# Gate halves copied out of PSUM between the silu groups, and the gated product written phase by phase

## The reference, cut to what matters

```python
h = rms_norm(x, mix_norm_g[l])
proj = h @ w_in[l]
a, gl, u_pool, g_conv, g_pool = jnp.split(proj, split_at, axis=-1)
yc = a * jax.nn.sigmoid(gl)                              # the gated product, 512 channels
yc = causal_dwconv(yc, conv_dw_w[l]) + conv_dw_b[l]      # 31 taps
yc = jax.nn.silu(layer_norm(yc, conv_ln_g[l], conv_ln_b[l]))
yc = yc @ w_conv_out[l]
zp = multiscale_pool(u_pool)
yp = jnp.einsum("bsgc,gcd->bsgd", zp, w_pool_grp[l]).reshape(b, s, d) * pool_scale[l]
merged = jax.nn.sigmoid(g_conv) * yc + jax.nn.sigmoid(g_pool) * yp
x = x + merged @ w_out[l]
```

## Time and profile before

| | us |
|---|---|
| median of three runs | 4167.49 |
| the three runs | 4167.48, 4446.34, 4167.49 |
| the profiled execution | 4192.85 |
| its slowest core (3), first to last instruction | 4191.3 |
| its other cores | 4155.9 to 4190.1 |
| TensorE busy | 3937.4 (94%) |
| VectorE busy | 2655.0 (63%) |
| ScalarE busy | 1983.3 (47%) |
| GpSimd busy | 203.6 (5%) |

### The profile page before, as it was taken

The page is one execution under the profiler, slowest core; times in us unless marked ns, Lnnn a source line. Parts: engine busy times, 40 slices in busy tenths (PEclk is TensorE's granted clock), DMA queues, the critical chain, the costliest instruction groups (busy, mean ns, idle before and its releaser), DMA issues.

```text
span 4191.3 us, 56900 instructions; the slowest of 8 cores (4155.9 to 4191.3 us)
## 1 busy us (share of the span) xinstructions
PE 3937.4 (94%) x18320; PEld 1797.1 (43%) x18320; DVE 2655.0 (63%) x3240; ACT 1983.3 (47%) x3793; POOL 203.6 (5%) x379
## 2 busy tenths in 40 slices
PE   6999999999999999989999999999999989999898
PEld 2444444444443444434444444444444434444343
DVE  4537775377764876548775387653867549665576
ACT  3445435454454543445444464434645445453544
POOL 1000001000000000000010000100000000000000
PEclk9899999999999999999999999999999999999999
DMA  6552353534752336333574434534257524352242
GB/s 129 111 91 49 67 94 71 91 53 78 145 126 51 66 64 106 66 55 52 101 153 101 85 52 80 94 65 85 51 111 141 105 44 76 67 98 53 53 76 68
DMA packets 108816, 348.20 MB, mean 83 GB/s; under 512 B 11888, under 2 KB 46960, under 8 KB 83952
## 3 DMA queue, kind: packets, MB, share of 16 engines
q0 software_dynamic: 41760, 275.11, 38.3%
q1 hardware_dynamic: 66768, 69.46, 6.2%
HBM read 586.05 MB, written 16.78 MB: 144 GB/s over the span
## 4 chain that ended last, share of the span: by engine, by line
PE 85%; ACT 6%; DVE 4%; issue 3%; DMA 1%; SPq 0%; DVEq 0%; ACTq 0%; POOLq 0%; POOL 0%
PE ps L424 85%; ACT F L397 2%; DVE H L411 2%; ACT AR L397 1%; ACT L397 1%; ACT RS L397 1%; DVE AR L728 1%; ACT SQ L397 1%; DVE X L401 1%; DMA AR<-xT 0%; DVE SQ L401 0%; ACT GB L397 0%; DMA RING<-wst 0%; DVE X L411 0%; DMA AR<-AR 0%
## 5 line engine op out<-in xcount | busy, mean ns | idle before, releaser
L424 PE MATMUL ps<-H,RING 128*128 128x512 bf16 x10240 | 2321.9, 386 | 97.9 <-DVE H L411 47.7
L424 PEld LDWEIGHTS ps<-H,RING 128*128 128x128 bf16 x10240 | 1012.1, 99 | 1366.4 <-issue 249.0
L424 PE MATMUL ps<-AR,RING 128*128 128x512 bf16 x4864 | 1085.1, 380 | 34.1 <-ACT RS L397 21.6
L397 ACT ACTIVATE AR<-ps 128x512 bf16<-128x512 f32 (+1 forms) x1024 | 602.6, 600 | 675.6 <-PE ps L424 648.4
L411 DVE SCALAR_TENSOR_TENSOR F<-AR,VEC,F 128x1024 f32<-128x1024 bf16 (+1 forms) x576 | 687.9, 1194 | 100.9 <-ACT F L397 58.2
L424 PEld LDWEIGHTS ps<-AR,RING 128*128 128x128 bf16 x4864 | 475.1, 98 | 614.9 <-issue 60.6
L401 DVE TENSOR_TENSOR X<-ps,X 128x512 f32<-128x512 f32 x512 | 341.4, 686 | 280.4 <-PE ps L424 280.4
L397 ACT ACTIVATE SQ<-X 128x512 bf16<-128x512 f32 x384 | 241.9, 631 | 575.0 <-DVE X L401 493.0
L397 ACT ACTIVATE GB<-ps 128x512 bf16<-128x512 f32 x320 | 184.0, 606 | 467.0 <-PE ps L424 466.2
L500 POOL DMA_DIRECT2D RING<-wst x280 | 149.0, 532 | 3687.3 <-PE ps L424 3667.9
L397 ACT ACTIVATE GB<-F 128x1024 bf16<-128x1024 f32 x192 | 189.4, 987 | 279.3 <-DVE F L411 278.4
(11 more groups left out here) (75 smaller groups left out, 2049.5 us busy)
## 6 DMA issues: line engine op xcount, KB each, us to landing
RING<-wst POOLq DMA_DIRECT2D x184, 1024.0 KB, 10.1
RING<-wst POOLq DMA_DIRECT2D x64, 704.0 KB, 8.4
RING<-wst POOLq DMA_DIRECT2D x32, 768.0 KB, 7.6
AR<-AR SPq DMA_DIRECT2D x256, 64.0 KB, 4.6
X<-xT SPq DMA_DIRECT2D x64, 256.0 KB, 14.2
yT<-X SPq DMA_DIRECT2D x64, 256.0 KB, 8.4
AR<-xT SPq DMA_DIRECT2D x40, 256.0 KB, 7.0
WX<-wst POOLq DMA_DIRECT2D x8, 1280.0 KB, 15.7
```

The costliest lines, as they stand in the source:

```text
L397: S.add("act", lambda h: h.activation(out=out.ap, in_=in_.ap, func=func, scale=s, **kw), reads=rd, writes=out.keys)
L424: S.add("pe", lambda h: h.matmul(out.ap, lhsT=lhsT.ap, rhs=rhs.ap, start=start, stop=stop), reads=lhsT.keys + rhs.keys, writes=out.keys)
```

## The change

There are two edits in the mixer.

The first changes the access patterns of the gated product (L725 to L727), and neither its inputs, its result nor its place. Before, the loops ran over n outside and the phase j inside: both inputs were read in order of position, and each of the 512 results was written 512 bytes from the one before it. Now j runs outside and n inside: the results are written in four runs of 128 neighbours, PSUM is read at every fourth float32 (16 bytes apart) and GB at every fourth bf16 (8 bytes apart).

The second moves gate halves q = 6 to 9 into the rounds of `ln_finish`. Behind the four silus and four DMAs of round r, the eight matmuls of q = 6 + r are recorded, and a Copy on ScalarE brings their bank as float32 into a half of F0 or F1 (`park`). Behind `ln_finish` four Sigmoids read the parked halves and write the same places of GB as before; then q = 10 to 15 follow as they did.

```diff
             def ev_gl(c):
                 def ev(s, ps):
                     ACT(sub(sgs[c], s), ps.v(), AF.Sigmoid)
-                    o_ap = GLU[c].ap.rearrange("p (j n) -> p n j", j=4)[:, s * 128:(s + 1) * 128, :]
-                    a_ap = psa[c].ap.rearrange("p (n j) -> p n j", j=4)
-                    g_ap = sub(sgs[c], s).ap.rearrange("p (n j) -> p n j", j=4)
+                    o_ap = GLU[c].ap.rearrange("p (j n) -> p j n", j=4)[:, :, s * 128:(s + 1) * 128]
+                    a_ap = psa[c].ap.rearrange("p (n j) -> p j n", j=4)
+                    g_ap = sub(sgs[c], s).ap.rearrange("p (n j) -> p j n", j=4)
                     S.add("dve", lambda h: h.tensor_tensor(out=o_ap, in0=a_ap, in1=g_ap, op=ALU.mult),
...
                         S.add("sp", lambda h, src=src, dst=dst: h.dma_start(out=dst, in_=src),
                               reads=YS[g].v().keys, writes=[("ACP", g)], dma_sem="ac%d" % g)
+                    gate_half(6 + q, GP[q])
+                    done.add(6 + q)
+
+            GP = [F[0].v(0, ST), F[0].v(ST, T), F[1].v(0, ST), F[1].v(ST, T)]
 
-            def gate_half(q):
+            def gate_half(q, park=None):
...
-                ACT(sub(gates[k], s), ps.v(), AF.Sigmoid)
+                if park is None:
+                    ACT(sub(gates[k], s), ps.v(), AF.Sigmoid)
+                else:
+                    ACT(park, ps.v(), AF.Copy)
+                    parked.append((sub(gates[k], s), park))
...
             ln_finish()
             if pstate.pop("x_pending", False):
                 unit_load(now["b"], hf)
-            for k in range(3, 8):
+            for o_, i_ in parked:
+                ACT(o_, i_, AF.Sigmoid)
+            for k in range(5, 8):
                 do_gate(k)
```

More of the change, by code:

```diff
@@ L862, in mixer @@
             done = set()
+            parked = []
             blk = ring_get(l, "upb")
```

## The result

| | before | changed |
|---|---|---|
| median, us | 4167.48 | 4203.0 |
| lowest and highest of the runs compared | 4166.86, 4167.49 | 4200.37, 4205.31 |
| slowest core of the profiled execution | 4191.3 (core 3) | 4203.8 (core 1) |
| waits of TensorE for the gates' sigmoid | 22.0 | none |
| waits of TensorE for the layer norm's DMAs | 1.8 | 61.3 |

The ratio is 1.0086, with a 95% interval of 1.0066 to 1.0105: 36 us slower, where 20 us less were forecast. Some executions of most kernels here, the profiled one of the kernel before with its stretch at a granted 0.81 among them, have two or four cores at a lower clock than the others; the times in this document are of executions in which all eight were alike, and so the two profiled spans differ by 12.5 us only while the runs give the 36.

A forecast was written before the change was run, and what follows sets the result against it. TensorE's chain of waits, 85% TensorE itself, was taken as the bound, with clock lost behind waits. Product 28.4 us gained, gate halves 2.1 - 4.0 - 6 = -8: 20 us off 4167.5 gives 4147 us, range 4129 to 4171.

The forecast's parts named there:

- the sentence on SP's queue: Eighth mixer, layer norm: SP's last DMA issue stays at 3772.4, lands at 3774.6; TensorE's wait moves there, 0.7 us gained.
- the clock at these places: New waits before the convolution's output, 3.0 to 4.5 us, over 5 in the fourth mixer: 6 us more charged for half clock.
- The bound at 2.43: Gated product on VectorE: 0.69 us taken; 2.43, no gain, if the new reads are as dear as the old writes.
- slower than before: Rival: strided reads hold the product up; edits cancel at 1.9 us, 4175 us at 2.43; chance 0.11, values between included.
- The last application: Even mixers: the layer norm's last application on VectorE ends at 606.14 instead of 609.24, 3.1 us earlier.
- its clock term: Even mixers: shorter half-clock stretch behind the waits gives back between 1.7 and 3.4 us a mixer, 2.55 taken.
- The product's edit: All mixers: even 22.6, first odd 2.6, bank waits of the others 3.2; 28.4 us gained, between 24 and 33.
- no table load: Rival: each Copy among the silus brings table loads on ScalarE, 10 us a mixer, 4217 us; chance 0.03. Forecast: 77 as before.
- The copies delay the last silu: Layer norm on ScalarE: four copies between silus make the last silu 1.5 us later, hidden behind SP's lag.
- The memory squares of the fourth mixer: First and fourth mixer: four copies in front on ScalarE make the squares 2.0 us later, twice, minus 4.0.
- the DMAs did not come earlier: Rival: SP issues at 0.55 us, not 0.79; last landing 2.7 us earlier in six mixers, 4131 us; chance 0.09.
- No gain, clock lost: Rival: new waits at the convolution's output all bring long slow stretches, about -20, against the product's gain; 4166 us, chance 0.15.

## Why the prediction was wrong

**The step that failed** is the sentence on SP's queue: "its last issue stays at 3772.4 and lands at 3774.6", and with it "the wait moves from the bank to the DMA, and 0.7 us is gained". The issue did stay. The landing did not: 6.9 to 8.6 us for the last four, instead of 2.2. The 2.2 were read from a stretch of the kernel before in which no weight load was in flight, and carried into one in which the edit itself puts a load of 1 MB there. The forecast followed the queues that the edit names, ScalarE's and SP's, and never asked what TensorE's earlier end of q = 15 sets free. In this kernel it frees a ring slot, and POOL's queue was waiting for nothing else: the row was in the timeline of the eighth mixer, 0.6 us after TensorE had ended q = 15. Holding this load back took 48 us off, halving it took 26: shown.

The price was in the trace of the kernel before as well. There the load that takes the slot of q = 7 is issued 3.6 us ahead of the first of the same 16 DMAs, and the first six of them take 5.1 to 7.1 us to land:

```profile
3756.74 0.53 POOL L500 DMA_DIRECT2D RING<-wst  x1 [26.94 <-PE ps L424]
```

```profile
L837 SPq DMA_DIRECT2D AR<-AR x6: 547/578/1611, 3760.3 to 3764.0; - x6
...
DMA to landing us min/median/max: 5.1/6.3/7.1
```

It cost nothing there, because the last of the 16, for which TensorE waits, come later. Over that whole trace the DMAs of L837 take 3.7 us in the median and up to 8.4.

**What followed from it** is the clock at these places, 6 us forecast. The waits went from 24 us (22.0 + 1.8) to 72 (61.3 + 10.5), and the half-clock time rose from 125 to 172 us where the product alone lowered it to 99. The halves cost 4227 - 4167.5 = 60 us. Some 41 to 46 are longer waits (68 against 27 in the median of the cores, 59.5 + 10.5 against 23.8 on core 3), and 13 are clock: TensorE works 125 us at half clock with the halves alone and 99 before. In the six mixers of the long waits the half-clock stretches of core 1 are 10.2 or 13.7 us; the part of them that lies in the wait costs nothing, as from 3782 to 3786. With the load held, TensorE works 92 us at half clock against 80 with the product alone, which is the 6 us that were forecast.

**Right in mechanism and near in size:**
- The product takes 0.69 us. The bound at 2.43 is out, and with it the rival "slower than before". What the Trainium skill ("Advanced Engine Details and Errata", section Memory Cachelines) says of PSUM lines of 8 bytes, it says of matmuls; PSUM read at a stride of 16 bytes and GB at 8 cost VectorE nothing that these rows show.
- The last application comes 3.3 us earlier (3.1 forecast), and the slow stretch at the start of the even mixers is nearly always gone, which is the upper bound of its clock term. The product's edit gave 25 us of 28.4: 15 of waits and 10 of clock, where 17 and 11 were reckoned.
- TensorE no longer stops before q = 14; no table load is added (77 as before).
- The copies delay the last silu by 1.2 us (9.42 from first start to last end against 8.20; 1.5 forecast), and SP's lag hides it.
- The memory squares of the fourth mixer start 1.9 us later behind the first silu (2.0 forecast), and the convolution's output 1.8 us later. TensorE waits 5.1 and 5.4 us for them in the first and fourth mixer.

One reading beside these was loose: the 16 issues of SP are not evenly spaced at 0.79 us. Most follow each other at 0.70 to 0.77, and one takes 1.6 us (2.1 in the changed kernel); 0.79 is their mean. The sum does not hang on it.

**The rivals.** The product alone did not turn out slow, no table load appeared, and the DMAs did not come earlier. "No gain, clock lost" had the right place and the wrong cause: it let the clock alone take the gain, to 4166 us. With the load held, when the waits are those that I had reckoned (22 us in six mixers, 3.1 to 4.5 each), the kernel takes 4155, against 4147 forecast and inside the range. Without the collision the sum was 8 us off, and the halves would still have lost: 12 us against the product alone, where 8 were forecast.

## What to carry to other kernels

When an edit lets an engine finish a block of work earlier, list what that end releases, the prefetch of the next weights above all, and look at what is in flight at the new time. A DMA's time to landing is a property of the stretch, not of the DMA: take it from a stretch with the same neighbours, or bound it by the landing of the largest load that can be in front. And where a wait is removed ahead of a DMA on the critical path, try first to hold the prefetch behind that DMA: here it brought no wait for weights. It repaired the collision and did not make the halves pay, since a wait of 3 us for the gates had only been exchanged for one of 3.1 to 4.5 us for the DMAs.

## What the runs showed of the hardware

- A 64 KB DMA inside the SBUF from SP's queue lands 2.2 us after issue with no weight load in front. Issued while a load of 1 MB from HBM is in flight on POOL's queue, it lands behind that load: 6.9 to 8.6 us behind one of 8.4, and 4.7 to 5.7 behind one of 512 KB that took 5.6. One issued 0.7 us ahead of the load still took 2.2.
- A VectorE product of 128x512 with a bf16 result takes 2.43 us when each result lies 512 bytes from the last, and 0.69 when the results are neighbours and the reads are strided: PSUM at 16 bytes, bf16 at 8.
- DMAs issued from POOL's queue land no later than those of SP's for these 64 KB copies: 2.2 us in the median against 2.7 in the eighth mixer, with the two queues side by side.
- A half-clock stretch costs only the work in it: the halves alone raised the half-clock time by some 60 us and TensorE's work in it by 26, which is 13 us of loss.
